# Splitting the three-level step of gated linear attention around the Hyena step

## The reference

```python
h = rmsnorm(x, norm_mix)
proj = jnp.einsum('btd,de->bte', h, w_in)
q, k, v, r, g_lr, hy_in = jnp.split(proj, np.cumsum(IN_SIZES)[:-1].tolist(), axis=-1)
o_gla = gla_group(q, k, v, r, g_lr, ...)   # 4 heads, a gated scan in each direction
o_hy = hyena_group(hy_in, ...)             # short conv, two long convolutions by FFT, gates
x = x + jnp.einsum('bte,ed->btd', jnp.concatenate([o_gla, o_hy], axis=-1), w_out)
h = rmsnorm(x, norm_ffn)
x = x + (jax.nn.silu(h @ w_gate) * (h @ w_up)) @ w_down
```

## Time and profile before

| | us |
|---|---|
| median of 3 runs | 1368.05 (1366.61 to 1368.76) |
| the profiled execution | 1361.24 |
| its span, first to last instruction | 1359.4 |
| TensorE matmuls busy | 1295.6 (95%) |
| GpSimd busy | 672.6 (49%) |
| ScalarE busy | 497.8 (37%) |
| VectorE busy | 465.9 (34%) |
| mean granted TensorE clock | 0.992 |

### The profile page before, as it was taken

The page is one execution under the profiler, slowest core; times in us unless marked ns, Lnnn a source line. Parts: engine busy times, 40 slices in busy tenths (PEclk is TensorE's granted clock), DMA queues, the critical chain, the costliest instruction groups (busy, mean ns, idle before and its releaser), DMA issues.

```text
span 1359.4 us, 20990 instructions
## 1 busy us (share of the span) xinstructions
PE 1295.6 (95%) x9056; PEld 1052.2 (77%) x9056; DVE 465.9 (34%) x637; ACT 497.8 (37%) x804; POOL 672.6 (49%) x395
## 2 busy tenths in 40 slices
PE   5999987999999999999999999889999999999997
PEld 5766776788888778888877877667888888888886
DVE  5865677525022220000058465566320000000003
ACT  4735443434222222212256635344333222322122
POOL 2654652472555445544426765226545555555441
PEclk9999999999999999999999999999999999999999
DMA  5211211123222222322212211112213223332322
GB/s 215 82 60 48 64 63 48 47 79 110 93 93 93 93 94 93 108 104 98 94 62 78 66 50 60 63 38 71 94 62 104 99 93 99 103 109 94 105 97 78
DMA packets 31196, 115.71 MB, mean 85 GB/s; under 512 B 3456, under 2 KB 3712, under 8 KB 30720
## 3 DMA queue, kind: packets, MB, share of 16 engines
q1 hardware_dynamic: 31104, 114.37, 25.0%
HBM read 112.26 MB, written 2.10 MB: 84 GB/s over the span
## 4 chain that ended last, share of the span: by engine, by line
PE 81%; DVE 13%; issue 2%; ACT 2%; POOL 1%; DMA 1%; POOLq 0%; SPq 0%; DVEq 0%; ACTq 0%
PE ps L1177 16%; PE ps L1179 16%; PE ps L1178 16%; PE ps L1199 6%; PE ps L1196 6%; PE ps L1197 6%; PE ps L1407 2%; PE ps L1393 2%; PE ps L1218 2%; PE ps L1193 2%; DVE spec L1038 2%; PE ps L1188 2%; PE ps L1190 2%; PE ps L1329 1%; PE ps L1268 1%
## 5 line engine op out<-in xcount | busy, mean ns | idle before, releaser
L743 POOL TENSOR_TENSOR w_lo<-w_raw,w_hi 128x1024 fp32r<-128x1024 f32 x192 | 470.4, 2450 | 494.8 <-ACT w_hi L437 494.7
L1177 PE MATMUL ps<-h_hi,w_hi 128*128 128x512 f32 (+1 forms) x1064 | 430.3, 404 | 1.1 <-DVE g L951 0.6
L1179 PE MATMUL ps<-h_hi,w_lo 128*128 128x512 f32 (+1 forms) x1064 | 414.2, 389 | 0.0
L1178 PE MATMUL ps<-h_lo,w_hi 128*128 128x512 f32 (+1 forms) x1064 | 413.6, 389 | 0.0
L437 ACT ACTIVATE w_hi<-w_raw 128x1024 fp32r<-128x1024 f32 x192 | 201.7, 1051 | 198.8 <-PE ps L1199 194.5
L1177 PEld LDWEIGHTS ps<-h_hi,w_hi 128*128 128x128 f32 x1064 | 200.8, 189 | 53.6 <-issue 10.6
L1178 PEld LDWEIGHTS ps<-h_lo,w_hi 128*128 128x128 f32 x1064 | 200.9, 189 | 44.9 <-issue 5.8
L1179 PEld LDWEIGHTS ps<-h_hi,w_lo 128*128 128x128 f32 x1064 | 200.4, 188 | 42.6
L1151 DVE TENSOR_TENSOR hid<-ps,sg 128x512 f32<-128x512 f32 x44 | 30.4, 692 | 421.9 <-PE ps L1179 421.9
L806 POOL TENSOR_TENSOR hid_lo<-hid,hid_hi 128x512 fp32r<-128x512 f32 x44 | 57.7, 1311 | 125.9 <-ACT hid_hi L721 125.9
L819 DVE TENSOR_TENSOR x<-x,ps 128x512 f32<-128x512 f32 x32 | 20.5, 682 | 256.4 <-PE ps L1193 252.2
(11 more groups left out here) (184 smaller groups left out, 1563.7 us busy)
## 6 DMA issues: line engine op xcount, KB each, us to landing
w_raw<-in_units SPq DMA_DIRECT2D x198, 512.0 KB, 3.4
gain<-in_gain SPq DMA_DIRECT2D x5, 512.0 KB, 4.7
par<-in_par SPq DMA_DIRECT2D x2, 1118.5 KB, 9.4
x<-in_x SPq DMA_DIRECT2D x4, 512.0 KB, 7.7
out_y<-x SPq DMA_DIRECT2D x4, 512.0 KB, 2.6
cst<-in_cst SPq DMA_DIRECT2D x1, 1024.0 KB, 13.6
cst<-in_cst SPq DMA_DIRECT2D x1, 224.0 KB, 3.6
mask_f<-in_mask SPq DMA_DIRECT2D x1, 160.0 KB, 11.8
```

The source lines that it names most:

```text
L743: nc.gpsimd.tensor_tensor(w_tile(g, 1), w_raw[:, g % RAW], w_tile(g, 0).bitcast(F32), ALU.subtract).then_inc(s_lo, 1)
L1177: nc.tensor.matmul(out, hi, act_hi, start=start, stop=False)
L1178: nc.tensor.matmul(out, hi, act_lo, start=False, stop=False)
L1179: return nc.tensor.matmul(out, lo, act_hi, start=False, stop=stop)
```

## The change

`level_step` is given the levels that it runs. Where the step has three masked levels, the first one (level 3, 32 matmuls) is run before the Hyena step, and levels 4 and 5 (64 matmuls) after everything else at the end of the slot. The first part waits for level 3's `xld` alone. The second part has its own waits for `xld` of level 5 and for `big`, and raises `pair`. Nothing is computed differently and no other step is moved.

```diff
-            def level_step(L, h, p):
-                pe.wait_ge(xld.sem, xld.at(L, lvl(h, STEPS[p][-1]) + 1))
+            def level_step(L, h, p, levels):
+                pe.wait_ge(xld.sem, xld.at(L, lvl(h, levels[-1]) + 1))
...
-                    for l in STEPS[p]:
+                    for l in levels:
...
-                last.then_inc(pair.sem, 1)
+                if levels[-1] == STEPS[p][-1]:
+                    last.then_inc(pair.sem, 1)
...
                     if hp:
-                        level_step(L, *hp)
+
+                        level_step(L, *hp, STEPS[hp[1]][:1] if hp[1] == 2 else STEPS[hp[1]])
...
                 if (slot, at) == (24, 1):
                     sum_square(L, 1)
+                if at == 1 and hp and hp[1] == 2:
+                    level_step(L, *hp, STEPS[2][1:])
```

## The result

The changed kernel takes 1355.6 us (median of 4 runs, 1355.29 to 1357.56), the kernel before 1367.6 us beside it: a ratio of 0.9915, with a 95% interval of 0.9898 to 0.9932. That is 12 us less; 10.9 were forecast. The profiled execution took 1355.79 us (span 1354.0), and that is only 5.4 us less than the profiled execution of the kernel before. Both numbers need an explanation: the moved steps give 10 to 10.7 us in the profiles, and what lies between that and either number is for the most part TensorE's clock in places that no edit touched.

The account below looks back on a forecast made before the run. TensorE's own instructions, busy 95% of the span, were taken as the bound. Gains of 5.7 + 1.8 + 0.8 + 1.0 + 1.6 = 10.9 us took the median of 1368.05 to 1357.2 us, range 1353.5 to 1364.

Parts of the forecast that it names:

- Instruction supply: Gaps in the three-level bursts, 9.8 us in 6 pieces: late refills of TensorE's instructions, about 3.5 us from their start.
- no effect: Rival, chance 0.07: the gaps aren't supply and stay, now inside the second part; 1368 us.
- slot 10 of layer 0: Burst at this slot's end: the Hyena step covers the refill; gain 1.9 us.
- slot 18: Bursts at this slot's end in both layers: the refill runs under the Hyena step; gain 1.9 us each.
- slots 14: Ends of these slots: gaps of 0.70 and 0.51 us vanish, less 0.2 each; gain 0.5 and 0.3.
- slot 10 of layer 1 with its clock: End of this slot: gap of 1.91 us covered, gain 1.8; no fall of the clock behind it, gain 1.6.
- slot 6: Layer 0: filter spectra's product runs before 64 matmuls, VectorE starts earlier, the 1.17 us wait at slot 7 goes; gain 1.0.
- The term of 1.6 us at layer 1's slot 10: Transform behind the gap: with no gap ahead the clock doesn't fall to 1.2 GHz; gain 1.6 us, bounds 0 and 1.6.
- it all shifts together: Whole kernel: every later step follows a slot's end, so the full 10.9 us comes through.
- the waits at L1407 stay as long: TensorE's waits at the inverse transform: as long as before, since the VectorE chains ahead start from TensorE's transforms.
- Swallowed: Rival, chance 0.12: what is won before slot 17 is lost in its wait for VectorE; gain 4 us, 1364.
- Slower: Rival, chance 0.05: gaps stay and meet the next slot, three more stretches at 1.2 GHz cost 4.9 us; 1373.

Follow-up runs that it names:

- The split alone: Against the kernel before: the three-level step issued as two calls (one level, two levels) back to back, the Hyena step behind both; 1367.24 us, ratio 1.0006.
- the Hyena step first: Against the changed kernel: the Hyena step stands ahead of all three masked levels, which then run in one burst; 1366.92 us, ratio 0.9999 to the kernel before.

## Why the prediction was right

**What the gap is.** Instruction supply was argued from two rows of the DMA view and the length of the burst. The runs show it by intervention: a shift of half a packet removes the gaps at slots 10 and 18 and makes others, a whole packet puts all six back, and every gap counted stands at one remainder by 256. The rival *no effect* leaned on the memory of 2048 instructions that the Trainium skill gives TensorE (Runtime: NRT & Kernel Launch, Instruction fetch mechanics). It is out: that figure and the measurement differ, and the measurement decides. The gaps behave as if only the packet after the one in use were ever ahead. The same section of the Trainium skill also says "The IRAM is only 2 cache lines" of 16 KiB, and that agrees with the traces; the forecast had used the figure of 2048 alone.

**Why the Hyena step covers it.** It was to run after the refill has begun and before the packet is needed. The split alone (10.8 us of gaps) and the Hyena step first (8.7) gain no time that can be measured, the changed kernel keeps 0.8 us of gaps.

**The terms**, forecast against the stretches of the table: slot 10 of layer 0, 1.9 against 1.8; slot 18, 1.9 against 1.5 and 1.6; slots 14, 0.5 and 0.3 against 0.6 and 0.4; slot 10 of layer 1 with its clock, 1.8 + 1.6 against 3.2; slot 6, 1.0 against 0.9. In sum 10.9 against 10.0. Two sizes were off. At slot 18 a remainder of the gap stays (0.41 in layer 0, where the forecast had the packet come in time). And slot 6's 1.0 did not last: the wait at slot 7 had covered the refill behind it, and 0.5 of it came back. The forecast named the stream's rule and did not ask which other refills it met once a wait was gone.

**The clock.** The term of 1.6 us at layer 1's slot 10 was right for the execution that was profiled, and its reason, the gap ahead, is borne out: six profiles keep the four long gaps (1.85 to 2.41 us), and 10 of these 24 are followed by half clock; in the seven profiles with slots 10 and 18 split, the granted clock is 1.00 at all 28 of these places, from the transform's first half to its second.

What failed is "so it all shifts together". The clock took back 3.8 us in the profiled execution, at both slots 20, at one slot 17 and at the start. With the refill behind slot 7 and the terms' 0.9 on top, 1355.8 us was measured where 1350.3 was expected of a profiled one. The forecast that the waits at L1407 stay as long failed too (11.7 to 9.5 us), for the reason given at slot 20.

In the timed runs the median moved by 12 us. The other executions of the kernel before are all slower than the first profiled one. The forecast left the 6.8 us between that profile and the median unexplained, and said that stops of this kind would enlarge the gain. The second profile supports that little: 0.8 of its 5.7 us are longer gaps, 3.4 are slot 24's clock. Against it the changed kernel's profile is 11.1 us shorter: about 10.7 from the stretches with a moved step, 3.1 from those with slot 24, and 2.8 lost again elsewhere. Slot 24's low clock stands in 8 of 12 places in the six profiles that keep the long gaps, and in 3 of 14 in the seven with slots 10 and 18 split; that the change brings this about isn't shown. So the mechanism and its size are right, and that the median was met within 1.6 us is in part luck: gains and losses of clock that the forecast didn't have nearly cancel. How they divide in the timed runs isn't shown, as those have no profile.

**The rivals.** *Swallowed* is out by the unchanged 8.7 us at L1305. *Slower* is out too, since the gaps didn't stay. Its mechanism is real: with the Hyena step first the gaps meet the next slot, and three of four are followed by half clock.

## What to carry to other kernels

An idle time in the middle of a burst of small instructions, for no semaphore, with a packet of the instruction queue beside it, was a late refill in every case here. To test for it, count instructions, not microseconds: the places stand at one remainder. It was mended by a few long instructions placed behind the point where the refill starts, and in part by shifting the stream by half a packet; but any edit that adds or removes instructions upstream moves all such places, so a gain of this kind should be checked against a shifted copy of both kernels, as was done here. One profiled execution can stand 6 us under a median of 1367: profile the baseline twice before a difference of two spans is read.

## What the runs showed of the hardware

- All 60 gaps of the 14 profiles stand at the same remainder by 256 instructions. One packet of 16 KB is fetched for 252 matmuls and loads, or 256 instructions with TensorE's semaphore instructions and drains counted (18418 in 72 packets). Where a packet was entered well inside a burst at a slot 10 or 18, the first instruction of the next one came 3.1 to 3.8 us later (layer 0's slot 10, kernel before: 118.35 to 121.94), and 1.2 to 1.6 us after its own packet had landed.
- 128 idle instructions made an unchanged order 6.9 us (0.5%) faster, 256 made it 0.4 us faster, which is no difference that can be measured.
- A gap of 1.9 to 2.4 us among small matmuls was followed by half clock in 10 of 24 places: the granted clock of 124.80 to 128.10 us is 0.50 in the second execution profiled of the kernel before (gap 2.14), and behind the gap of 2.32 in the first it stayed full. Which it will be, nothing here lets one say ahead.
